# Gate weight tiles between the attention's steps in a two-layer mixer kernel on one Trainium2 core

## What is computed

```
h = rmsnorm(x); proj = h @ w_in
sb_q, sb_k, sb_v, fx_q, fx_k, fx_v, f_logit, m_q, gate_logit = split(proj)
o_sb  = stick_breaking_attention(...)   # 8 heads of 64
o_fox = forgetting_attention(...)       # 8 heads of 64
o_mem = memory_attention(...)           # 4 heads of 128
gates = sigmoid(gate_logit.reshape(b, s, 3, 1024))
merged = gates[0] * (o_sb @ w_branch_sb) + gates[1] * (o_fox @ w_branch_fox)
         + gates[2] * (o_mem @ w_branch_mem)
x = x + merged @ w_out
```

## Time and profile before

| | us |
|---|---|
| median of 3 runs (2092.24 to 2098.1) | 2092.77 |
| the profiled execution, its own time | 2093.24 |
| its span in the profile | 2091.4 |
| outside the span | 1.84 |

### The profile page before, as it was taken

The page is one execution under the profiler, slowest core; times in us unless marked ns, Lnnn a source line. Parts: engine busy times, 40 slices in busy tenths (PEclk is TensorE's granted clock), DMA queues, the critical chain, the costliest instruction groups (busy, mean ns, idle before and its releaser), DMA issues.

```text
span 2091.4 us, 26737 instructions
## 1 busy us (share of the span) xinstructions
PE 2015.3 (96%) x9652; PEld 1654.2 (79%) x9652; DVE 1508.3 (72%) x1344; ACT 1254.8 (60%) x1093; POOL 40.7 (2%) x86
## 2 busy tenths in 40 slices
PE   7999999998899999999999999999999988999999
PEld 6888877886688888878888788887867767888887
DVE  5554565775788888888888888888886646556554
ACT  5544566222576777777677776777765566445442
POOL 0000001001000000000000000000001100000000
PEclk9999999998899999999999999999999987999999
DMA  9544630003599989999899998998965400555540
GB/s 364 196 177 151 221 132 30 1 1 151 209 357 347 356 345 347 348 351 367 332 355 344 348 357 353 343 356 346 360 234 228 180 22 1 202 179 184 199 172 30
DMA packets 72662, 500.77 MB, mean 239 GB/s; under 512 B 7824, under 2 KB 10128, under 8 KB 12944
## 3 DMA queue, kind: packets, MB, share of 16 engines
q1 hardware_dynamic: 72448, 499.30, 63.0%
q10 hardware_dynamic: 144, 0.52, 0.1%
HBM read 498.74 MB, written 1.05 MB: 239 GB/s over the span
## 4 chain that ended last, share of the span: by engine, by line
PE 75%; DVE 6%; ACT 3%; issue 2%; POOL 1%; DVEq 0%; ACTq 0%; POOLq 0%
PE bank L738 15%; PE bank L739 15%; PE bank L743 15%; PE bank L467 6%; PE bank L468 6%; PE bank L476 6%; PE bank L527 3%; PE bank L717 2%; PE bank L772 1%; PE bank L766 1%; POOL small L1596 1%; DVE w_lo L1652 1%; DVE kT L1732 0%; PE bank L492 0%; PE bank L604 0%
## 5 line engine op out<-in xcount | busy, mean ns | idle before, releaser
L1973 DVE TENSOR_TENSOR w_lo<-raw,w_hi 128x2048 fp32r<-128x2048 f32 x339 | 771.5, 2290 | 126.8 <-ACT w_hi L1325 121.8
L1325 ACT ACTIVATE w_hi<-raw 128x2048 fp32r<-128x2048 f32 x339 | 649.9, 1918 | 166.8 <-PE bank L743 166.7
L1652 DVE TENSOR_TENSOR w_lo<-raw,w_hi 128x2048 fp32r<-128x2048 f32 (+2 forms) x136 | 297.3, 2197 | 168.0 <-ACT w_hi L1173 167.1
L1173 ACT ACTIVATE w_hi<-raw 128x2048 fp32r<-128x2048 f32 (+2 forms) x136 | 249.0, 1840 | 193.9 <-PE bank L476 187.7
L738 PE MATMUL bank<-w_hi,xT 128*128 128x512 f32 x896 | 360.3, 402 | 4.5 <-ACT w_hi L1325 4.5
L739 PE MATMUL bank<-w_hi,xT 128*128 128x512 f32 x896 | 351.8, 393 | 0.0
L467 PE MATMUL bank<-w_hi,xT 128*128 128x512 f32 (+1 forms) x784 | 310.6, 398 | 19.2 <-DVE xT L2249 8.4
L468 PE MATMUL bank<-w_hi,xT 128*128 128x512 f32 (+1 forms) x784 | 307.4, 394 | 0.0
L743 PE MATMUL bank<-w_lo,xT 128*128 128x512 f32 x896 | 242.5, 393 | 0.0
L738 PEld LDWEIGHTS bank<-w_hi,xT 128*128 128x128 f32 x896 | 169.1, 189 | 41.4 <-ACT w_hi L1325 4.7
L743 PEld LDWEIGHTS bank<-w_lo,xT 128*128 128x128 f32 x896 | 168.8, 188 | 37.1
(11 more groups left out here) (391 smaller groups left out, 2074.3 us busy)
## 6 DMA issues: line engine op xcount, KB each, us to landing
raw<-in_experts_dram SPq DMA_DIRECT2D x339, 1024.0 KB, 4.9
raw<-in_tiles_dram SPq DMA_DIRECT2D x125, 1024.0 KB, 4.8
raw<-in_tiles_dram SPq DMA_DIRECT2D x9, 512.0 KB, 3.5
row<-in_rows_dram SPq DMA_DIRECT2D x1, 1040.0 KB, 18.5
h<-in_x_dram SPq DMA_DIRECT2D x1, 1024.0 KB, 10.6
pool_m<-in_pool_mix_dram SPq DMA_DIRECT2D x1, 1024.0 KB, 16.4
mem_in<-in_mem_dram SPq DMA_DIRECT2D x2, 512.0 KB, 5.1
out_dram<-h SPq DMA_DIRECT2D x2, 512.0 KB, 2.9
```

What stands on the lines that cost most here:

```text
L1173: nc.scalar.activation(w_hi[:, i % SPL, 0:kc * w], raw[:, i % RAW, 0:kc * w], ACT.Copy)\
L1325: nc.scalar.activation(w_hi[:, j % SPL, :], raw[:, j % RAW, :], ACT.Copy).then_inc(m_hi, 1)
L1652: nc.vector.tensor_tensor(w_lo[:, i % SPL, 0:kc * w], raw[:, i % RAW, 0:kc * w], w_hi[:, i % SPL, 0:kc * w], ALU.subtract).then_inc(split_ ...
L1973: nc.vector.tensor_tensor(w_lo[:, j % SPL, :], raw[:, j % RAW, :], w_hi[:, j % SPL, :], ALU.subtract).then_inc(m_lo, 1)
```

## The change

The number of raw buffers in the dense parts falls from 7 to DENSE = 4 (loads, landed semaphores, both splits); the experts keep 7. `heads_in` moves from `w_lo` into the three raw buffers that are no longer used there, and DVE's limit goes. In the stream all six gate blocks stand before the six branch blocks, in the order of GATES, and the branches run 2, 1, 0 (mem, fox, sb). PE multiplies one gate tile at the end of every odd step u up to 21, eleven in all; the twelfth stands between the transpositions of the outputs. ACT and DVE split one tile in each odd step, and ACT computes a gate in steps 5, 9, 13, 17 and 21. All six gates are kept, in `xn` and in four places of their own, so the semaphore `merged` goes.

```diff
+DENSE = 4
+GATES = ((2, 0), (2, 1), (1, 0), (1, 1), (0, 0), (0, 1))
...
     for name, c0 in B_IN:
         put(block(("b_in", name), "w_in_2", c0, CB, D))
+    for b, c in GATES:
+        put(block(("b_gate", b, c), "w_in_2", 3592 + b * D + c * CB, CB, D))
     for c in range(2):
-        for b, w in enumerate(("sb", "fox", "mem")):
-            put(block(("b_gate", b, c), "w_in_2", 3592 + b * D + c * CB, CB, D))
-            put(block(("branch", b, c), f"w_branch_{w}_2", c * CB, CB, CB))
+        for b in (2, 1, 0):
+            put(block(("branch", b, c), f"w_branch_{('sb', 'fox', 'mem')[b]}_2", c * CB, CB, CB))
...
         raw = sb("raw", [P, RAW, KC * CB])
+        spare = nc.sbuf_base - 4 * KC * CB * (RAW - DENSE)
         w_hi = sb("w_hi", [P, SPL, KC * CB], FR)
         low_parts = nc.sbuf_base
         w_lo = sb("w_lo", [P, SPL, KC * CB], FR)
 
-        heads_in = nc.alloc_sbuf_tensor_at("heads_in", [P, 8, 6 * P], F32, offset=low_parts)
+        heads_in = nc.alloc_sbuf_tensor_at("heads_in", [P, 8, 6 * P], F32, offset=spare)
         cst = sb("cst", [P, N_CONST])
...
         oT2 = [at(f"oT2_{b}", [P, 4, S], 20 + 8 * b, FR) for b in range(3)]
-        gate2 = at("gate2", [P, NT, CB], 8)
+        gates = {(2, 0): xn[:, :, 0:CB], (2, 1): xn[:, :, CB:D]}
+        for (b, c), off in zip(GATES[2:], (48, 40, 12, 8)):
+            gates[b, c] = at(f"gate{b}{c}", [P, NT, CB], off)[:, :, :]
...
+                def gate_tile(k):
+                    name = ("b_gate",) + GATES[k // 2]
+                    if k % 2 == 0:
+                        begin(name, "A")
+                    tile(name, k % 2, xT1, xT2)
+
+                def turn_output(br):
+                    o, kind, hh = ((o_sb, "sb", 7), (o_fox, "fx", 7), (o_mem, "mm", 3))[br]
+                    result(("out", HEADS2.index((kind, hh))))
                     for j in range(2):
                         b = tp_bank(("oT", br, j), "D")
                         for k in range(2):
...
+                for u in range(len(HEADS2) + 4):
+                    for do, v in ((scores, u), (second, u - 2), (output, u - 4)):
+                        if 0 <= v < len(HEADS2):
+                            do(v)
+                    if u % 2 and u < 22:
+                        gate_tile(u // 2)
+                turn_output(2)
+                turn_output(1)
+                gate_tile(11)
+                turn_output(0)
                 for c in range(2):
-                    for br in range(3):
-                        if c or br:
-                            gemm(("b_gate", br, c), "A", xT1, xT2)
+                    for br in (2, 1, 0):
                         result(("oT", br, 1))
-                        if (br, c) == (2, 1):
+                        if (br, c) == (0, 1):
                             turn_norm("mg", xn, (0,), (xn_done, 5))
                         gemm(("branch", br, c), "D", oT1[br], oT2[br])
...
-                    if i >= RAW:
-                        sp.wait_ge(split_lo, i - RAW + 1)
-                    sp.dma_start(raw[:, i % RAW, 0:kc * n], src).then_inc(landed[i % RAW], 16)
+                    if i >= DENSE:
+                        sp.wait_ge(split_lo, i - DENSE + 1)
+                    sp.dma_start(raw[:, i % DENSE, 0:kc * n], src).then_inc(landed[i % DENSE], 16)
...
-                sp.wait_ge(split_lo, max(i for i in range(NA) if i % RAW == j) + 1)
+                if j < DENSE:
+                    sp.wait_ge(split_lo, max(i for i in range(NA) if i % DENSE == j) + 1)
                 load_expert(j, 0)
...
+                def gate(br, c):
+
+                    banks = after(("b_gate", br, c))
+                    for tt in range(NT):
+                        tell(nc.scalar.activation(gates[br, c][:, tt, :], banks[tt][:, :], ACT.Sigmoid,
+                                                  scale=root("m2", tt)), acc_free["A"] if tt else a_own)
+
+                def turn_output(br):
+                    for j in range(2):
+                        b = batch(("oT", br, j))
+                        tell(nc.scalar.activation(oT1[br][:, 2 * j:2 * j + 2, :],
+                                                  b[:, :].rearrange("p (a b) -> p a b", a=2), ACT.Copy), hi_out)
+
+                gate0 = cbs[("b_gate",) + GATES[0]][0]
                 for u in range(len(HEADS2) + 3):
                     for do, v in ((softmax_exp, u - 1), (sb_exp, u - 3), (scores, u), (turned, u - 2)):
                         if 0 <= v < len(HEADS2):
                             do(v)
-                split_to(group_of["b_gate", 0, 0][1] + SPL - 1)
-                for br in range(3):
-                    for j in range(2):
-                        b = batch(("oT", br, j))
-                        tell(nc.scalar.activation(oT1[br][:, 2 * j:2 * j + 2, :],
-                                                  b[:, :].rearrange("p (a b) -> p a b", a=2), ACT.Copy), hi_out)
-                last_branch = None
-                for c in range(2):
-                    for br in range(3):
-                        banks = after(("b_gate", br, c))
-                        if last_branch:
-                            act.wait_ge(acc_free["D"], group_of[last_branch][3])
-                            act.wait_ge(merged, last_branch[1] + 3 * last_branch[2] + 1)
-                        last_branch = ("branch", br, c)
-                        for tt in range(NT):
-                            tell(nc.scalar.activation(gate2[:, tt, :], banks[tt][:, :], ACT.Sigmoid,
-                                                      scale=root("m2", tt)), acc_free["A"] if tt else a_own)
-                end = group_of["branch", 2, 1][1]
+                    if u % 2 and u < 22:
+                        split_to(gate0 + u // 2 + SPL)
+                    if u % 4 == 1 and u > 4:
+                        gate(*GATES[u // 4 - 1])
+                turn_output(2)
+                turn_output(1)
+                gate(*GATES[5])
+                turn_output(0)
+                end = group_of["branch", 0, 1][1]
+                split_to(end + 1)
                 norm_turn("mg", None, halves=(0,))
                 split_to(end + 3)
...
+
+                gate0 = cbs[("b_gate",) + GATES[0]][0]
+                for u in range(len(HEADS2) + 5):
+                    for do, v in ((weights, u - 4), (output, u - 5), (scores, u), (softplus, u - 1), (second, u - 2)):
+                        if 0 <= v < len(HEADS2):
+                            do(v)
+                    if u % 2 and u < 22:
+                        split_to(gate0 + u // 2 + SPL)
+                turn_output(2)
+                turn_output(1)
+                split_to(gate0 + 11 + SPL)
+                turn_output(0)
                 for c in range(2):
-                    for br in range(3):
-                        if (br, c) == (2, 1):
-                            split_to(group_of["branch", br, c][1])
+                    m = [xn[:, tt, c * CB:c * CB + CB] for tt in range(NT)]
+                    for br in (2, 1, 0):
+                        if (br, c) == (0, 1):
+                            split_to(group_of["branch", br, c][1] + 1)
                             norm_turn("mg", None, halves=(0,))
                         banks = after(("branch", br, c))
                         dve.wait_ge(acc_free["A"], group_of["b_gate", br, c][3])
-                        m = [xn[:, tt, c * CB:c * CB + CB] for tt in range(NT)]
+                        gate = [gates[br, c][:, tt, :] for tt in range(NT)]
                         for tt in range(NT):
-                            o = gate2[:, tt, :] if br else m[tt]
-                            tell(nc.vector.tensor_tensor(o, banks[tt][:, :], gate2[:, tt, :], ALU.mult),
+                            tell(nc.vector.tensor_tensor(gate[tt], banks[tt][:, :], gate[tt], ALU.mult),
                                  acc_free["D"] if tt else d_own)
-                        if br:
+                        if br < 2:
                             for tt in range(NT):
-                                tell(nc.vector.tensor_tensor(m[tt], m[tt], gate2[:, tt, :], ALU.add),
-                                     d_own if tt == 0 else xn_done if br == 2 else d_own)
-                        tell(nc.vector.memset(small[:, 70:71], 0.0), merged)
+                                tell(nc.vector.tensor_tensor(m[tt], m[tt], gate[tt], ALU.add),
```

More of the change, by code:

```diff
@@ L338, in build @@
         x_split = sem("x_split")
-        landed = [sem(f"landed{i}") for i in range(RAW)]
+        landed = [sem(f"landed{i}") for i in range(DENSE)]
         split_hi = sem("split_hi")
@@ L389, in build @@
         relu_sq = sem("relu_sq")
-        merged = sem("merged")
         small_act = sem("small_act")
@@ L940, in output @@
                     last.then_inc(tp_done, 1)
-                for u in range(len(HEADS2) + 4):
-                    for do, v in ((scores, u), (second, u - 2), (output, u - 4)):
-                        if 0 <= v < len(HEADS2):
```

(21 more changed lines are left out.)

5 lines of the change are left out of this document (3 added, 2 removed).

## The result

| | before | changed |
|---|---|---|
| median of the runs, us | 2093.76 (5 runs) | 2082.57 (5 runs, 2079.93 to 2084.6) |
| the profiled execution, us | 2093.24 | 2081.59 |
| its span, us | 2091.4 | 2079.5 |
| ratio of the times, 95% interval | | 0.9946 (0.9933 to 0.9958) |

A forecast was written before the change was run, and what follows sets the result against it. PE was taken to bound the kernel, with time to win only where it waits or runs slowly. Attention 120.4 plus 44 us after it, 164.4 for 191.7, saves 27.3 us: 2093.24 - 27.3, so 2066 us; range 2058 to 2084.

The forecast's parts named there:

- PE's work of the attention: Attention: 54.8 us for the heads at full clock plus 60.4 for eleven moved tiles, at least 115.2 us.
- After the attention: From the attention's end to the last branch tile: 41.9 us of PE work plus 2 for last outputs, 44 us.
- The ring of four: Dense parts: loads into four raw buffers stay hidden, 0 us lost, with 12 us as the bound.
- the paragraph on DVE: Attention: DVE's 25.2 us more are hidden; softmax and sb scores, splits and reading take at most 10.9 of 11 us.
- the attention's term: Attention: 120.4 us, ACT's work plus all its idle time, the upper of two ends, 115.2 and 120.4.
- (B): Attention: splits and ACT's gates lengthen the heads' chain; attention 147.5 us, kernel 2093, nothing gained; chance 0.05.
- (A): Attention: PE's clock stays low in the heads' part, 17.3 us come back, kernel 2083; chance 0.19.
- (C): Attention: PE's tiles stand on the heads' chain too, so the kernel is slower, 2113 us; chance 0.06.
- (D): Start of the kernel: the ring of four starves PE, up to 12 us, kernel 2078; chance 0.07.
- The prediction is wrong if ACT's idle grows: Attention: sign against the forecast, if ACT's idle time, 21.2 us before, grows rather than shrinks.
- The case of the forecast itself: Whole kernel: time between 2058 and 2074 us, with PE's new work covering the heads' chain; chance 0.63.
- The rule against the change: ACT in the attention: by the Trainium skill six added table switches cost 8.3 us more, kernel 2074; not used.

The follow-up runs named there:

- e7: Changed kernel with DVE's split one pair later and PE's gate tile between scores(u) and second(u - 2): 2065.53 us, ratio 0.9863.
- e4: Kernel before, with the ring of four raw buffers in the dense parts as the only change: 2092.96 us against 2093.72, ratio 1.0002.
- e2: Changed kernel, but DVE splits in each odd step the tile that ACT split one pair of steps before: 2071.58 us, ratio 0.9899.
- e9: Changed kernel, but ACT splits at the start of odd steps, ahead of its work for the heads: 2070.84 us, ratio 0.9891.
- e6: Changed kernel with DVE's split one pair later and softplus before the reading of scores in even steps: 2063.43 us, ratio 0.9852.
- e8: e2 with the gates as plain copies, without the sigmoid and six table loads of the attention: 2070.92 us, ratio 0.9896.
- e1: Changed kernel, but in even steps DVE computes softplus(u - 1) before it reads the scores of step u: 2080.7 us, ratio 0.9943.

## Why the prediction was right or wrong

**What held.** PE's work of the attention: 115.2 us forecast, 116.8 worked out for the changed kernel, 116.5 read in e7 at a clock of 1.00. So both readings behind it hold, 54.8 us for the heads at full clock and 5.49 us for each tile. ACT's busy time: 99.2 forecast, 99.08 measured, table loads included. DVE's: 81.6 and 80.26. After the attention: 44 forecast, 42.3 measured, with no wait of PE for the last outputs, for which 2 us had been added; the branch tiles follow each other at 5.5 us, and DVE's 5.1 us for each are covered. The ring of four: nothing, shown by e4 alone. PE waits for ACT 1.8 us in all.

**The step that failed** is the paragraph on DVE, and through it the attention's term: 120.4 us forecast, 139.7 measured. It said that from one pair to the next "three things must fit: ACT's softmax and sb scores, both splits, and DVE's reading", 10.9 us at most in 11: "it fits, with little to spare". The measured time follows from this one term: 2065.9 + 19.3 in the attention - 1.7 behind it - 2.2 ahead of it is 2081.3, and the profiled execution took 2081.59. The paragraph added up durations of one path. It did not ask, for each instruction that is put into a queue, what stands behind it, and from when the one that it waits for can run:

1. DVE's split waits for ACT's, which stands last in ACT's step. The forecast named this wait and what is queued behind it, but only the reading of the fx scores; it missed the sb weights (L2182, L2183), which PE needs before that. The wait is 29.0 us of DVE; taking it away shortened the attention by 11.5 us (e2) and 8.6 us (e9), the medians by 11.0 and 11.7.
2. PE's own tile stands between the sb scores and the next fx scores. DVE's reading of the fx scores can't start before the tile is done, and the softplus, whose input is there, stands behind the reading. The forecast's 2.1 us were for the reading alone; with the maxima and the softplus, which the sum didn't have, DVE takes 3.5. That makes a loop of tile 5.5, scores 2.5, DVE 3.5 and second with output 1.8 us, 13.3 us a pair at full clock; e2's tiles are 13.3 us apart. The forecast had 11. e6 and e7 loosened it in two ways and took another 5.2 and 7.2 us off e2's attention.

After both, 139.7 - 11.5 (e2) - 7.2 (e7) = 121.0 us are left. That PE waits for DVE's softplus in this software pipeline could have been read before: 6.1 us in 6 times, against the 6.3 us for ACT on which the forecast built.

**The rivals.** (B), the splits on the chain of the heads, is what happened in part, though ACT's gates and their loads, which it counted too, are not on it (e8). It was priced as if every split were on the chain; the measured loss is 19.3 us of attention over the forecast for its 27. (A), the low clock, stands there with 8.4 us for its 17.3, but as a consequence: with the gaps filled the clock is 0.99 to 1.00 and nothing remains of it (e2, e6, e7). That its time, 2083, is the measured one within 1 us is luck: the rest of the loss is waits for DVE, where (A) had named a looser coupling of ACT and PE. (C) and (D) did not happen. Of the signs that the forecast gave, PE busy over 95% of the attention failed (90%), the clock near 1.00 failed (0.94), PE's waits for ACT held. "The prediction is wrong if ACT's idle grows" was the right alarm on the wrong engine: ACT's idle did grow, from 21.2 to 139.7 - 99.1 = 40.6 us, and all that it shows is that ACT was not what the chain waited for.

**The weights.** The case of the forecast itself had a chance of 0.63 on an argument that was tight by 0.1 us in 11. An upper bound of a path that is equal to the time at hand is no reason for such a chance; the range held the time only because (A) was taken in, so by luck and not by the mechanism.

**The rule against the change.** Between e2 and e8 six table loads less in the attention (146 and 140 instructions of ACT) and the shorter copies are 8.2 us of ACT's busy time; six loads of 1.28 us are 7.7 of it. The drain of 1.38 us beside each load, which the Trainium skill states (ScalarE: Activation LUTs, What ACT_TABLE_LOAD costs), shows in no row here: where the changed kernel has the load of a gate at 1714.45 us, its end is at 1715.73 and the gate's first instruction starts at 1715.75; nor is it ahead of the load, since ACT's split ends at 1714.43. By the Trainium skill the added loads were the danger. By e8 the six that it saves cost the kernel nothing.

## What to carry to other kernels

When filler work goes into the gaps of a pipeline of in-order engines, write down for each inserted instruction what it waits for, and for each instruction behind it who waits for that; a sum of durations that fits says nothing on this. Let the second half of a two-engine job (here the remainder after the rounding) run one round behind the first. And when two waits lie in the same loop, a single edit can measure as nothing and be worth 5 us after the other one is made (e1 and e6): test them together before dropping either.

## What the runs showed of the hardware

A gap doesn't always bring the low clock. In the changed kernel PE is idle from 1790.4 to 1792.3 us, and the clock falls:

```profile
1791.00:1792.00 1.00, 0.00 (x0) 0.00 (x0) 0.93 (x3) 0.91 (x3) 0.00 (x0) 1.00 0.00 0
1792.00:1793.00 1.00, 0.73 (x3) 0.62 (x4) 0.90 (x4) 0.94 (x4) 0.00 (x0) 0.81 0.00 0
1793.00:1794.00 1.00, 1.00 (x7) 1.00 (x5) 0.63 (x3) 0.95 (x3) 0.00 (x0) 0.50 0.00 0
...
1796.00:1797.00 1.00, 1.00 (x6) 0.83 (x5) 0.00 (x0) 1.00 (x1) 0.00 (x0) 0.98 0.00 0
```

In e2 the same place has the same gap, from 1782.1 to 1784.0 us, and the clock stays:

```profile
1782.00:1783.00 1.00, 0.08 (x1) 0.00 (x0) 0.90 (x4) 0.23 (x1) 0.00 (x0) 1.00 0.00 0
1783.00:1784.00 1.00, 0.03 (x1) 0.03 (x1) 0.90 (x4) 0.94 (x5) 0.00 (x0) 1.00 0.00 0
1784.00:1785.00 1.00, 1.00 (x7) 0.95 (x8) 0.90 (x4) 0.94 (x3) 0.00 (x0) 1.00 0.00 0
```

What tells the two apart isn't settled. A low stretch just before is not it: the next gap of the changed kernel, from 1805.3 to 1807.2 us, is as long, comes 9 us after the low stretch of 1793 to 1796, and the clock stays:

```profile
1806.00:1807.00 1.00, 0.00 (x0) 0.00 (x0) 0.93 (x3) 0.96 (x4) 0.00 (x0) 1.00 0.00 0
1808.00:1809.00 1.00, 1.00 (x11) 1.00 (x10) 0.90 (x4) 0.95 (x3) 0.00 (x0) 1.00 0.03 8
```

And in e9 three gaps of 1.9 us leave the clock alone and the fourth brings it down. A low stretch costs 1.6 us in its pair in the changed kernel (14.9 for 13.3) and 3.0 in e9 (16.3 for 13.3). No run was made on that.
